# Four blocks of the down product per tile at its end, its last block in slots of its own, and another order of VectorE's steps between two layers

## The reference

```python
def hybrid_layer(x, ...):                                    # twice
    proj = x @ w_in                                          # 1024 x 2336
    ... three kinds of attention ...
    h = layer_norm(DEEPNORM_ALPHA * x + heads @ w_o, ln1_g, ln1_b)
    ffn = (jax.nn.silu(h @ w_gate) * (h @ w_up)) @ w_down    # inner width 2816
    return layer_norm(DEEPNORM_ALPHA * h + ffn, ln2_g, ln2_b)

def second_block(x, c, w_ada, ...):                          # once
    mod = (c_act @ w_ada[l] + b_ada[l])[:, None, :]          # 1024 x 6144, one row of c
    sh_m, sc_m, ga_m, sh_f, sc_f, ga_f = jnp.split(mod, 6, axis=-1)
    h = _rms_norm(x, g_pre_mix[l]) * (1.0 + sc_m) + sh_m
    y = _hybrid_mixer(h, ...)                                # begins with h @ w_in, 1024 x 2544
    x = x + ga_m * _rms_norm(y, g_post_mix[l])
    h = _rms_norm(x, g_pre_ffn[l]) * (1.0 + sc_f) + sh_f
    return x + ga_f * _rms_norm(_swiglu(h, ...), g_post_ffn[l])
```

## Time and profile before

| what | us |
|---|---|
| median of three runs | 1055.68 |
| lowest and highest run | 1054.01 and 1056.41 |
| the profiled execution's own time | 1057.2 |
| its span, first to last instruction | 1055.4 |
| TensorE matmul busy | 995.3 |
| VectorE busy | 715.6 |
| ScalarE busy | 514.7 |

### The profile page before, as it was taken

How to read it: one execution, slowest core, us unless ns; L and a number is a source line. 1 busy time by engine, 2 the same in 40 slices (tenths; PEclk the granted TensorE clock), 3 DMA queues, 4 the chain that set the end, 5 groups by cost and what they waited for, 6 DMA issues and landing times.

```text
span 1055.4 us, 14488 instructions
## 1 busy us (share of the span) xinstructions
PE 995.3 (94%) x5600; PEld 849.8 (81%) x5600; DVE 715.6 (68%) x1276; ACT 514.7 (49%) x897; POOL 48.0 (5%) x70
## 2 busy tenths in 40 slices
PE   6999989999999899999999999789998979999997
PEld 6878768888888898777888888678776768888886
DVE  3665677888785765668878786756777366666543
ACT  3455525555522456634655533355476266556531
POOL 5100020000000200011000000100000000000000
PEclk9999999999999999999999999989999989999999
DMA  8642429978694563246988776365221127666541
GB/s 289 213 138 80 120 77 283 270 215 273 211 351 132 161 189 117 81 120 184 288 235 248 252 290 235 111 199 169 80 81 41 40 63 214 179 185 199 186 173 40
DMA packets 191699, 184.97 MB, mean 175 GB/s; under 512 B 7130, under 2 KB 161013, under 8 KB 191632
## 3 DMA queue, kind: packets, MB, share of 16 engines
q1 hardware_dynamic: 188576, 175.85, 53.5%
q0 software_dynamic: 2768, 7.87, 2.5%
q10 hardware_dynamic: 288, 0.33, 0.1%
HBM read 182.97 MB, written 1.06 MB: 174 GB/s over the span
## 4 chain that ended last, share of the span: by engine, by line
PE 77%; DVE 12%; ACT 6%; issue 2%; POOL 1%; DMA 1%; SPq 0%; DVEq 0%; POOLq 0%; ACTq 0%
PE ps L1083 24%; PE ps L1035 15%; PE ps L1085 10%; DVE wl L1779 3%; PE ps L1013 3%; PE ps L1015 3%; PE ps L1014 3%; PE ps L1412 2%; PE ps L1118 2%; ACT probs L1548 2%; ACT wh L1524 2%; PE ps L1082 2%; PE ps L1171 1%; PE ps L1149 1%; PE ps L990 1%
## 5 line engine op out<-in xcount | busy, mean ns | idle before, releaser
L1779 DVE TENSOR_TENSOR wl<-raw,wh 128x2048 fp32r<-128x2048 f32 (+5 forms) x143 | 310.4, 2173 | 93.5 <-ACT wh L1524 93.2
L1083 PE MATMUL ps<-xhl,wh 128*128 128x512 f32 (+1 forms) x1040 | 358.5, 399 | 3.3 <-DVE xhl L1797 1.9
L1524 ACT ACTIVATE wh<-raw 128x2048 fp32r<-128x2048 f32 (+5 forms) x143 | 260.3, 1820 | 166.5 <-PE ps L1035 108.3
L1085 PE MATMUL ps<-xhl,wl 128*128 128x256 f32 (+1 forms) x910 | 254.8, 280 | 0.0
L1083 PEld LDWEIGHTS ps<-xhl,wh 128*128 128x128 f32 x1040 | 189.6, 191 | 38.5 <-DVE xhl L1797 2.3
L1085 PEld LDWEIGHTS ps<-xhl,wl 128*128 128x128 f32 x910 | 174.1, 191 | 5.2
L1862 DVE TENSOR_TENSOR scratch<-ps,scratch 128x256 f32<-128x256 f32 x132 | 55.7, 422 | 58.0 <-ACT scratch L1705 58.0
L1711 ACT ACTIVATE scratch<-scratch 128x256 f32<-128x256 f32 x66 | 27.7, 419 | 137.1 <-DVE scratch L1862 137.0
L1013 PE MATMUL ps<-wh,xhl 128*128 128x384 f32 (+4 forms) x204 | 74.5, 365 | 12.5 <-DVE wl L1779 7.3
L1035 PE MATMUL ps<-wh,gh 128*128 128x512 f32 x264 | 84.1, 392 | 0.0
L1035 PE MATMUL ps<-wl,gh 128*128 128x512 f32 x264 | 83.4, 390 | 0.0
(11 more groups left out here) (277 smaller groups left out, 1432.4 us busy)
## 6 DMA issues: line engine op xcount, KB each, us to landing
raw<-in_w_down SPq DMA_DIRECT2D x33, 1024.0 KB, 5.0
adaw<-in_w_ada SPq DMA_DIRECT2D x24, 1024.0 KB, 7.5
raw<-in_w_gate SPq DMA_DIRECT2D x44, 512.0 KB, 4.1
raw<-in_w_up SPq DMA_DIRECT2D x44, 512.0 KB, 5.8
raw<-in_w_gate_up SPq DMA_DIRECT2D x44, 512.0 KB, 5.2
raw<-in_w_in SPq DMA_DIRECT2D x12, 768.0 KB, 4.7
raw<-in_w_in SPq DMA_DIRECT2D x8, 1024.0 KB, 5.1
raw<-in_w_o SPq DMA_DIRECT2D x8, 1024.0 KB, 4.9
```

Source lines behind the costliest of these rows:

```text
L1083: ins = mm(o, a[:, v, k, :], xhl[:, :, k, c], start=k == 0, stop=k == KC - 1)
L1085: mm(o[:, 0, :], b[:, v, k, :], xh[:, k, c], start=False, stop=False)
L1524: me.go(activation(halves(item)[0][:, 0:n], raw[:, ITEM[item] % NRAW, 0:n], ACT.Copy), wh_ready)
L1779: me.go(V.tensor_tensor(lo[:, 0:n], raw[:, ITEM[item] % NRAW, 0:n], hi[:, 0:n].bitcast(F32), ALU.subtract), wl_ready)
```

## The change

`TAIL` is 4: items 7 to 10 of the down product are taken for tile 0 first and then for tile 1. Item 10 gets slots of its own (`late`, in the place of `adaw`), so it is not in the ring, and the next layer's first three `win` items take the slots of `dn` 7, 8 and 9. In layers 0 and 1 the split of item 10 waits until all modulation steps of the layer are done, in layer 2 for the end of the output product. The last `ada` of a layer stands after `dn` 6, not after `dn` 7. In `to_win` VectorE splits item 1 ahead of tile 0's columns, and item 2 ahead of tile 1's `norm_rows` as before. Ahead of layer 2, the first half of tile 1's sums and statistics also stands ahead of tile 0's columns. ScalarE splits items 1 and 2 ahead of tile 0's columns.

```diff
-ADA_DN = {2: 3, 4: 4, 7: 5}
-TAIL = 3
+ADA_DN = {2: 3, 4: 4, 6: 5}
+TAIL = 4
...
-OWN = [k for L in range(2) for k in (("wo", L, 3), ("gu", L, 0))]
+OWN = [k for L in range(2) for k in (("wo", L, 3), ("gu", L, 0))] + [("dn", L, FC // 2 - 1) for L in range(3)]
...
+        late = [at("late_hi", [P, SLOTW], F32R, base + 8 * FC * S), at("late_lo", [P, SLOTW], F32R, base + 8 * FC * S + 4 * SLOTW)]
...
         def wait_slot(eng, item):
 
             if item in OWN:
-                wait_full(eng, ("s", item[1], 19) if item[0] == "gu" else ("o", item[1], 2, 1))
+                if item[0] != "dn":
+                    wait_full(eng, ("s", item[1], 19) if item[0] == "gu" else ("o", item[1], 2, 1))
+                elif item[1] < 2:
+                    eng.wait_ge(ada_summed, 12 * (item[1] + 1))
+                else:
+                    wait_full(eng, ("y", 2, 1, 1))
...
             def to_win(L):
 
                 start(split, "win", L, 0, 1)
-                for t in range(TT):
-                    if L == 2:
-                        square_rows("in", t)
-                    if t == 0:
-                        start(split, "win", L, 1, 2)
-                    columns("xT", L, t)
-                    if t == 0:
-                        start(split, "win", L, 2)
+                if L == 2:
+                    square_rows("in", 0)
+                start(split, "win", L, 1)
+                columns("xT", L, 0)
+                if L == 2:
+                    square_rows("in", 1)
+                columns("xT", L, 1)
...
             def to_win(L):
 
-                for t in range(TT):
-                    if L:
-                        norm_stats(L - 1, "d", 2, t)
-                        if t == 1:
-                            start(split, "win", L, 2)
-                        norm_rows(L - 1, 2, t)
-                    if L == 2:
-                        if t == 0:
-                            start(split, "win", L, 0, 1)
-                        mean_rms(t, "in", 1)
-                        dve.wait_ge(ev("rstd_in"), t + 1)
-                        for h in range(2):
-                            n = slice(512 * h, 512 * h + 512)
-                            me.go(V.tensor_scalar(z[:, t, n], x[:, t, n], rs[:, t, 1:2], D ** 0.5, ALU.mult, ALU.mult), ev("norm_in", 1))
-                    elif L and t == 0:
-                        start(split, "win", L, 0, 1)
-                    columns("xT", L, t)
-                    if t == 0:
-                        start(split, "win", L, 1, 2)
+                norm_stats(L - 1, "d", 2, 0)
+                norm_rows(L - 1, 2, 0)
+                start(split, "win", L, 0, 1)
+                if L == 2:
+                    pre_norm(0)
+                start(split, "win", L, 1, 2)
+                if L == 2:
+                    sums_half(1, "d", 1, 0)
+                    columns("xT", 2, 0)
+                    sums_half(1, "d", 1, 1)
+                    variance(1, 2, 1)
+                else:
+                    columns("xT", L, 0)
+                    norm_stats(L - 1, "d", 2, 1)
+                start(split, "win", L, 2)
+                norm_rows(L - 1, 2, 1)
+                if L == 2:
+                    pre_norm(1)
+                columns("xT", L, 1)
```

More of the change, by code:

```diff
@@ L798, in halves @@
             if item in OWN:
-                hi, lo = first if item[0] == "gu" else own
+                hi, lo = {"gu": first, "wo": own, "dn": late}[item[0]]
                 return hi[:, :], lo[:, :]
@@ L1797, in columns @@
                     me.go(V.tensor_tensor(b, v, a.bitcast(F32), ALU.subtract), cols_ready)
-            def norm_stats(L, unit, ln, t):
-                for h in range(2):
[L1802 to L1807, removed]
+            def sums_half(L, unit, t, h):
+                key = (unit, L, t, h)
+                wait_full(dve, key)
+                xs = x[:, t, 512 * h:512 * h + 512]
+                me.empty(V.scalar_tensor_tensor(out=xs, in0=xs, scalar=ALPHA, in1=ps[:, U.bank[key], :], op0=ALU.mult, op1=ALU.add), key)
+                me.settle()
+                me.go(V.bn_stats(st[:, t, h, :], xs))
+            def variance(L, ln, t):
                 me.settle()
@@ L1811, in norm_stats @@
                 me.go(V.tensor_scalar(va[:, t, 0:1], mv[:, t, 1:2], 1e-5, None, ALU.add), ev("var", ln, L))
+            def norm_stats(L, unit, ln, t):
+                for h in range(2):
+                    sums_half(L, unit, t, h)
+                variance(L, ln, t)
             def norm_rows(L, ln, t):
@@ L1896, in to_gates, with pre_norm @@
                 start(split, "gu", L, 1)
-            def to_win(L):
-                for t in range(TT):
-                    if L:
-                        norm_stats(L - 1, "d", 2, t)
-                        if t == 1:
-                            start(split, "win", L, 2)
-                        norm_rows(L - 1, 2, t)
-                    if L == 2:
-                        if t == 0:
-                            start(split, "win", L, 0, 1)
-                        mean_rms(t, "in", 1)
-                        dve.wait_ge(ev("rstd_in"), t + 1)
-                        for h in range(2):
-                            n = slice(512 * h, 512 * h + 512)
-                            me.go(V.tensor_scalar(z[:, t, n], x[:, t, n], rs[:, t, 1:2], D ** 0.5, ALU.mult, ALU.mult), ev("norm_in", 1))
-                    elif L and t == 0:
-                        start(split, "win", L, 0, 1)
-                    columns("xT", L, t)
-                    if t == 0:
-                        start(split, "win", L, 1, 2)
+            def pre_norm(t):
+                mean_rms(t, "in", 1)
+                dve.wait_ge(ev("rstd_in"), t + 1)
+                for h in range(2):
+                    n = slice(512 * h, 512 * h + 512)
+                    me.go(V.tensor_scalar(z[:, t, n], x[:, t, n], rs[:, t, 1:2], D ** 0.5, ALU.mult, ALU.mult), ev("norm_in", 1))
+            def to_win(L):
+                norm_stats(L - 1, "d", 2, 0)
[17 more added lines that the diff above has]
+                columns("xT", L, 1)
             def outputs(L, g):
```

## The result

| | before | with the change |
|---|---|---|
| median of 14 runs each, us | 1056.30 | 1049.42 |
| lowest and highest | 1054.01, 1059.39 | 1046.65, 1054.73 |
| profiled execution: time, span, mean granted clock | 1057.2, 1055.4, 0.982 | 1050.87, 1049.0, 0.986 |

The ratio is 0.9939 (95% interval 0.9929 to 0.9949), so 6.4 us faster, 5.4 to 7.5 us by the interval. The forecast was 4.57 us less, 1051.1 us. The direction holds; the size is a question.

What follows compares the result with a forecast made beforehand. The prediction took TensorE to bound the kernel (77% of the chain); 1.07 + 3.50 = 4.57 us off 1055.68 gave 1051.1 us. Its own range was 1050.2 to 1052.3 us, for 8 in 10 1049.0 to 1054.0 us.

Steps and rivals of the forecast that it cites:

- The wait before the last sum: Before the last `ada` in layers 0 and 1, TensorE waits for VectorE's last modulation steps: 0.73 us lost each.
- Item 10 in its own slots costs nothing: Down product's end: item 10's split is ready at 329.3, TensorE wants it at 332.3, 3.0 us to spare.
- ScalarE's columns fit behind the split of item 2: Layer changes: ScalarE's split ends at 345.0, tile 0's columns are wanted at 345.3; then 673.6 against 674.0.
- Rival C: Layer changes: ScalarE's split of item 2 comes late and delays columns, 1.5 us a place at most; 1052.6 to 1054.1 us; 8%.
- Ahead of layer 1: End of layer 0: item 1's split moves into VectorE's idle time, 1.80 less 0.73 us: 1.07 us gained.
- Ahead of layer 2: End of layer 1: 1.59 + 1.32 + 1.32 - 0.73 = 3.50 us gained on VectorE's path.
- early half: Ahead of layer 2: tile 1's first half of sums and statistics goes into VectorE's idle time before the columns: 1.32 us.
- the wait before the transposes: End of layer 1: four items at the end remove TensorE's wait before tile 0's transposes, 1.32 us.
- Nothing at the end of the kernel: Last layer: splitting off four items is worth nothing, since the end chain begins with tile 1's sums.
- Rival A: After the change of layer at 690 to 700, the lower clock goes away, 1.8 us more: 1049.3 us; 15%.
- the granted clock has other low stretches than before: Layers 1 and 2: other low stretches of the granted clock than before would show the prediction wrong; no size given.

Runs made afterwards that it cites:

- the last two filled kernels: The change with filler matmuls in TensorE's waits, 1044.32 us, and the same with the last modulation sum after item 7 of tile 0, 1042.52 us.
- the filled pair: The kernel before and the change, each with filler matmuls in TensorE's waits at layer changes and layer middles: 1048.77 us and 1044.32 us.
- the down product alone: Kernel before with only four items at the end, item 10's own slots and the last sum after item 6; old order between layers: ratio 1.0021.
- both orders: Kernel before with VectorE's and ScalarE's new order between the layers, on the old down product: ratio 1.0005 to before.
- VectorE's order: Kernel before with only VectorE's new order between the layers, old down product and ScalarE's old order: ratio 0.9964 to before.

## Why the prediction was right, and what it missed

Point by point, by its own steps:

- **The wait before the last sum**: 0.73 us reckoned for each layer. Measured 322.89 - 322.29 = 0.60 us and 648.87 - 648.27 = 0.60 us. Taking the wait away gave 0.64 us each in the profiles of the last two filled kernels, so both cost 1.2 to 1.3 us, a little less than the 1.46 us of the sum. The 1.8 us between their medians hold 0.6 us of clock.
- **Item 10 in its own slots costs nothing**: right (ready at 328.9; TensorE's first matmul with it is at 332.08).
- **ScalarE's columns fit behind the split of item 2**: right, by 0.31 and 0.45 us. Rival C did not come. What it rested on is real: with the split bound to the end of the product, ScalarE's order cost 4.3 us between the medians.
- **Ahead of layer 1**: 1.07 us reckoned, 1.13 us in the profile. TensorE's wait before item 2 had been given as about 0.7 us, and is 0.37 us. That was a slip in the sum: the old wait of 2.19 us, less the 1.07 us gained and the 0.73 us by which TensorE comes later, is 0.39 us.
- **Ahead of layer 2**: 3.50 us reckoned, 3.56 us in the profile; its parts 1.32 us (early half) and the wait before the transposes show singly. The waits of tile 1 stay at 2.72 and 2.08 us, as said.
- **Nothing at the end of the kernel**: right; the chain there begins with tile 1's sums as before.
- **Rival A** (the low clock ahead of layer 2 goes away, 1049.3 us) gave the measured time, but not by its mechanism. The low stretch is there in both profiles of the change, in the first at 0.78, 0.50 and 0.70 from 680 to 695. By these shares it lasts about 10 us, where before it lasted 6.8 us. The Trainium skill (TensorE: Matmul & The Clock Gate, Part 1) has the gate choose one of two rates by how busy TensorE has recently been, and calls the moment variable between runs. The rows agree with both: no stretch holds less than 0.50, and the same wait at the middle of layer 1 is followed by 0.66 in one execution and by 1.00 in another.

So the steps were right, 4.57 us reckoned and 4.69 and 4.74 us measured, and it is partly luck that the median lies in the range. The range for 8 in 10 reached down to 1049.0 us only to take in rival A, whose mechanism did not come. One of the prediction's own signs of being wrong did come: the granted clock has other low stretches than before. The profile of before has them from 485 to 490 and from 785 to 799; the first of the change has neither, the second has one from 480 to 490. What such a stretch costs depends on what stands in it. The one of before from 785 to 799 cost nothing against the change's profile, which has full clock there.

The term that was mis-sized is therefore the one that stood outside the sum. The forecast took the granted clock as equal on both sides and gave a change of it only to rivals. Measured, it is not equal: 0.9855, 0.9859 and 0.9857 over 28, 17 and 9 runs of before, 0.9884 and 0.9900 over 14 and 5 of the change. A difference of 0.003 to 0.004 over 1050 us is 3 to 4 us of full-speed time, of which some falls into waits. At 0.6 us for each 0.001, the 0.0029 between 0.9855 and 0.9884 are an estimated 1.7 us, near the 1.9 us by which the gain exceeds the forecast. That this extra part is the clock is shown by the filled pair, where it is gone. It goes with how much TensorE waits: the mean clock is 0.9829 with the down product alone, 0.9845 with both orders, 0.9871 with VectorE's order and 0.9878 to 0.9900 in the change and the kernels nearest to it. Which of the waits gives it was not settled. The single wait ahead of layer 1 did not (no effect in the kernel before), but with the down product alone, which has the same wait there, the clock fell behind it and all runs together were 2.2 us slower. One profiled execution per kernel is too few to tell where a stretch is low more often.

## What to carry to other kernels

When an engine is late at a hand-over, look for its idle time just before the place and move into it whatever it does behind: two splits and half a norm, moved by a few microseconds, gave nearly all of 4.7 us. Such an order needs its inputs early, and in a ring of slots this can hang on one item: with item 10 in the ring, ScalarE's early split took back the whole gain of VectorE's order; with slots of its own for item 10, it cost nothing. If TensorE's waits are short but many, compare the granted clock over all runs before explaining the last 2 us from one profile, and try filler matmuls in the waits: they gave more here (7.5 to 7.9 us in the kernel before) than the change itself. One should then compare two filled kernels place by place.

## What was not expected of the hardware

Filler matmuls, which compute nothing that is used, made the kernel before 0.7% faster, though the other engines' work stayed as it was. Behind TensorE's waits of 1.4 to 2.7 us its clock was at 1.2 GHz for 3 to 10 us, in some executions and not in others; in the profiles with fillers these places kept 1.00. Most of the spread of the runs went with it: 0.7 to 1.6 us remained with fillers. The Trainium skill (TensorE: Matmul & The Clock Gate, HAM oscillation) describes the same loss for a kernel that waits for its loads again and again; here the waits were for VectorE, and shorter.
